# The feed-forward layer of a transformer block by seven products of two-by-two blocks, with its activations kept in DRAM

## The chip, the cores and the metric

The kernel runs on one core of one Trainium2 chip. The metric is the device time of one execution in microseconds (us), the median over several runs.

## What is computed

One encoder layer on x, 512 rows by 2048 columns of float32. First comes attention with forget gates: a normalisation, a projection to q, k, v of 16 heads, per head the scores, a softmax and a weighted sum, and an output projection that is added to x. The result is called x1. The layer then ends with the part that the change is about:

```python
def swiglu(h, w_gu, w_down):
    gu = jnp.einsum('bsd,df->bsf', h, w_gu)          # 512x2048 by 2048x11264
    gate, up = gu[..., :D_FF], gu[..., D_FF:]        # D_FF = 5632
    return jnp.einsum('bsf,fd->bsd', jax.nn.silu(gate) * up, w_down)   # by 5632x2048

h = rmsnorm(x1, ffn_norm_g)
x = x1 + swiglu(h, w_gu, w_down)
```

## The kernel before

All products of matrices are made of three matmuls each. Every float32 operand is split into a rounded part ("hi", type fp32r) and the rest ("lo"), and `three` (L378 to L384) adds hi by hi, hi by lo and lo by hi in PSUM. ACT makes the hi parts of the weights (`split_hi`, L638), DVE the lo parts (`split_lo`, L868: raw minus hi). SP loads the raw weights, 1 MB at a time, into two slots (`load`, L200).

The work is staged in chunks of 4 weight units of 1 MB. After the 16 heads come four chunks of the output projection (d = 0 to 3), each of which ends in `x1_add` (L1030), where DVE adds the product to x in the tile `rows`. In the last of them PE transposes x1 (`transpose_rows`, L418) for the feed-forward. ACT takes sums of squares of x1 (`x1_squares`, L667) for the second normalisation. Its factors are brought to a row by two small matmuls (`rms_b`).

The feed-forward goes through the 5632 hidden columns in NP = 11 parts of 512. For each part there is a gate chunk into the PSUM banks G, an up chunk into the banks X, and a down chunk, which multiplies the part by 512 rows of w_down and adds the result to `rows` (`down_add`, L1085). The gate and up chunks give the hidden values transposed (weights stationary, activations moving), so no transposes are needed between. A gate chunk is scaled on DVE (L1068), put through silu on ACT (L796), scaled on POOL (L369), multiplied by up on DVE (L1076) and split again (L800, L1080). All this runs in a loop, in an order that is written out by hand per engine: each chunk has 16 steps s, and the splits and readers are placed at fixed steps. Each engine waits on semaphores for exactly what it reads. `w_lo_done` lets PE start a unit, and lets SP overwrite the raw slot.

A matmul streams 512 columns past 128 stationary ones. The feed-forward has 11 x 2 x 4 x 4 x 4 x 3 = 4224 of them for gate and up and 11 x 4 x 4 x 4 x 3 = 2112 for down, together 6336.

## Time and profile before

| | |
|---|---|
| median of 3 runs | 2278.01 us (2276.91 to 2278.36) |
| span of the profiled execution, first to last instruction | 2275.4 us |
| around the span, against the median | 2.6 us |
| PE busy | 2266.8 us, 11022 matmuls |
| PE weight loads | 1978.8 us |
| DVE busy | 904.3 us |
| ACT busy | 635.9 us |
| POOL busy | 225.6 us |
| DMA | 222.95 MB, 98 GB/s over the span |

The profile names the profiled execution's span and not its whole time. The median stands 2.6 us above the span, and this is taken as what lies around it. PE means TensorE's matmuls and PEld its weight loads, which overlap them. A busy PE is not PE at its peak, since the ends of matmuls are modelled; what counts is the distance from one start to the next. Lines such as L868 are lines of the kernel, and "out<-in" names the tile written and those read.

### The profile page before, as it was taken

The page shows a single profiled execution, that of the slowest core. Times are in us where ns is not written, and L with a number is a line of the kernel's source. Part 1 is how long each engine was busy: PE and PEld are TensorE (multiplying, and loading weights), DVE is VectorE, ACT ScalarE, POOL GpSimd, SP SyncE. Part 2 cuts the span into 40 slices and gives each one's busy share as a digit, 9 for nine tenths or more (in the row PEclk, how much of TensorE's full clock was granted, in tenths as well). Part 3 has the DMA queues.
Part 4 walks back from the last instruction along what each step waited for, and adds up shares of the span by engine and source line. Part 5 has one row for each costly group of instructions (what it writes and reads, how often), then busy time and mean ns, then how long its engine had stood idle before and what let it go on. Part 6 is the DMA issues. An engine that isn't in the chain of part 4 may idle for free.

```text
span 2275.4 us, 29033 instructions
## 1 busy us (share of the span) xinstructions
PE 2266.8 (100%) x11022; PEld 1978.8 (87%) x11022; DVE 904.3 (40%) x1553; ACT 635.9 (28%) x986; POOL 225.6 (10%) x395
## 2 busy tenths in 40 slices
PE   9999999999999999999999999999999999999999
PEld 8999999999988888888888888888888888888887
DVE  4544444444552242342433333342333334343334
ACT  5433333333442232222222121222222121222211
POOL 1322222222210000000000000000000000000000
PEclk9999999999999999999999999999999999999999
DMA  6333323333252223232232223222222223222223
GB/s 174 85 93 88 92 74 93 87 92 85 81 181 85 101 78 108 81 105 98 87 110 92 92 92 111 92 92 102 84 96 104 97 87 111 92 92 95 95 104 111
DMA packets 190548, 222.95 MB, mean 98 GB/s; under 512 B 8194, under 2 KB 106532, under 8 KB 190516
## 3 DMA queue, kind: packets, MB, share of 16 engines
q1 hardware_dynamic: 190304, 222.49, 30.1%
q8 instruction: 22, 0.36, 0.1%
q14 instruction: 10, 0.08, 0.0%
q10 hardware_dynamic: 212, 0.03, 0.0%
HBM read 218.26 MB, written 4.23 MB: 98 GB/s over the span
## 4 chain that ended last, share of the span: by engine, by line
PE 99%; DMA 0%; DVE 0%; ACT 0%; issue 0%; DVEq 0%
PE gemm L382 17%; PE gemm L384 17%; PE gemm L383 17%; PE aux L383 15%; PE aux L384 15%; PE aux L382 15%; PE aux L446 1%; PE aux L418 1%; PE aux L427 0%; PE aux L428 0%; DMA rows<-in_x 0%; DVE act_lo L873 0%; PE aux L493 0%; PE aux L492 0%; DVE w_lo L868 0%; PE aux L484 0%
## 5 line engine op out<-in xcount | busy, mean ns | idle before, releaser
L868 DVE TENSOR_TENSOR w_lo<-w_raw,w_hi 128x1024 fp32r<-128x1024 f32 (+1 forms) x424 | 483.7, 1154 | 843.0 <-ACT w_hi L638 843.0
L638 ACT ACTIVATE w_hi<-w_raw 128x1024 fp32r<-128x1024 f32 (+1 forms) x424 | 403.3, 988 | 1124.4 <-PE aux L384 650.7
L382 PE MATMUL gemm<-w_hi,act_hi 128*128 128x384 f32 (+2 forms) x1280 | 450.4, 352 | 1.6 <-DVE w_lo L868 1.6
L384 PE MATMUL gemm<-w_hi,act_lo 128*128 128x384 f32 (+2 forms) x1280 | 444.0, 347 | 0.0
L383 PE MATMUL gemm<-w_lo,act_hi 128*128 128x384 f32 (+2 forms) x1280 | 443.9, 347 | 0.0
L382 PE MATMUL aux<-w_hi,work_r 128*128 128x512 f32 x704 | 274.1, 389 | 0.1
L382 PE MATMUL gemm<-act_hi,w_hi 128*128 128x512 f32 x704 | 274.0, 389 | 0.0
L384 PE MATMUL gemm<-act_hi,w_lo 128*128 128x512 f32 x704 | 273.9, 389 | 0.0
L383 PE MATMUL aux<-w_lo,work_r 128*128 128x512 f32 x704 | 273.9, 389 | 0.0
L384 PE MATMUL aux<-w_hi,work_r 128*128 128x512 f32 x704 | 273.9, 389 | 0.0
L382 PE MATMUL aux<-act_hi,w_hi 128*128 128x512 f32 x704 | 273.9, 389 | 0.0
L383 PE MATMUL aux<-act_lo,w_hi 128*128 128x512 f32 x704 | 273.9, 389 | 0.0
L384 PE MATMUL aux<-act_hi,w_lo 128*128 128x512 f32 x704 | 273.9, 389 | 0.0
L383 PE MATMUL gemm<-act_lo,w_hi 128*128 128x512 f32 x704 | 273.9, 389 | 0.0
L382 PEld LDWEIGHTS gemm<-w_hi,act_hi 128*128 128x128 f32 x1280 | 241.0, 188 | 12.5 <-issue 2.0
L383 PEld LDWEIGHTS gemm<-w_lo,act_hi 128*128 128x128 f32 x1280 | 241.1, 188 | 10.4
L384 PEld LDWEIGHTS gemm<-w_hi,act_lo 128*128 128x128 f32 x1280 | 240.7, 188 | 10.0
L1085 DVE TENSOR_TENSOR rows<-aux,rows 128x512 f32<-128x512 f32 x176 | 121.6, 691 | 223.7 <-PE aux L384 223.7
L369 POOL TENSOR_TENSOR work<-work,rms_b 128x512 f32<-128x512 f32 x44 | 57.0, 1294 | 1241.6 <-ACT work L796 1241.6
L382 PEld LDWEIGHTS aux<-w_hi,work_r 128*128 128x128 f32 x704 | 132.1, 188 | 28.2 <-DVE work_r L1080 0.8
L384 PEld LDWEIGHTS aux<-act_hi,w_lo 128*128 128x128 f32 x704 | 132.1, 188 | 27.5
L384 PEld LDWEIGHTS gemm<-act_hi,w_lo 128*128 128x128 f32 x704 | 132.1, 188 | 27.5
(110 smaller groups left out, 1910.3 us busy)
## 6 DMA issues: line engine op xcount, KB each, us to landing
w_raw<-in_ffn_w_gate_up SPq DMA_DIRECT2D x88, 1024.0 KB, 4.8
w_raw<-in_fox_w_in SPq DMA_DIRECT2D x192, 256.0 KB, 3.3
w_raw<-in_ffn_w_down SPq DMA_DIRECT2D x44, 1024.0 KB, 4.9
w_raw<-in_fox_w_out SPq DMA_DIRECT2D x16, 1024.0 KB, 4.9
rows<-in_x SPq DMA_DIRECT2D x8, 1024.0 KB, 7.4
c_key<-c_scratch SPq DMA_DIRECT2D x16, 256.0 KB, 3.2
out_y<-rows SPq DMA_DIRECT2D x3, 1024.0 KB, 4.2
out_y<-rows SPq DMA_DIRECT2D x4, 256.0 KB, 2.3
```

Of the source, the lines that this page charges most:

```text
L369: g.tensor_tensor(silu_t[:, j], silu_t[:, j], rms2_b[:], ALU.mult).then_inc(silu_scaled, 1)
L382: mm(out, a_hi, b_hi, start=first, stop=False)
L383: mm(out, a_hi, b_lo, start=False, stop=False)
L384: return mm(out, a_lo, b_hi, start=False, stop=last)
L418: last = nc.tensor.transpose(X[i][:, bass.ts(t, P)], rows[:, kg, t, bass.ts(i, P)], ident[:])
L446: last = nc.tensor.transpose(dst[:, bass.ts(i - j, P)], prob[:, OFF[i] + P * j:OFF[i] + P * (j + 1)], ident[:])
L638: a.activation(w_hi[:, j % 2, k, 0:width], w_raw[:, j % 2, k, 0:width], ACT.Copy)\
L868: v.tensor_tensor(w_lo[:, j % 2, k, 0:width], w_raw[:, j % 2, k, 0:width], f32(w_hi[:, j % 2, k, 0:width]), ALU.subtract).then_inc(w_lo_do ...
L1085: v.tensor_tensor(rows[:, d, t, :], X[t][:], rows[:, d, t, :], ALU.add).then_inc(bank_free, 1)
```

## The change

The feed-forward is written anew; attention and the output projection stay as they were, but for where their tiles lie.

Both products are cut in two by two blocks: A (activations) in two halves of rows (256) and two halves of the inner dimension, B (weights) in two halves of the inner dimension and two of columns (gate and up for the first product). Instead of eight block products there are seven, in Winograd's form of Strassen's way. With the sums S1 = A21-A22, S2 = S1-A11, S3 = A11-A21, S4 = A12+S2 and T1 = B11+B12, T2 = T1+B22, T3 = B12+B22, T4 = T2+B21, the products are P1 = A11 B11, P2 = A12 B21, P3 = S4 B22, P4 = A22 T4, P5 = S1 T1, P6 = S2 T2, P7 = S3 T3, and the four result blocks are sums of them.

The work is a list `UNITS` of 264 units in 17 rounds, written out without loops. Rounds 0 to 10 make gate and up for 512 hidden columns each; rounds 11 to 16 make down, in three blocks of 8, 7 and 7 steps of the hidden dimension and two halves of columns. A round goes twice over its 8 (or 7) steps of the inner dimension. In the first pass (g = 0) a unit has 3 products and loads 3 blocks of weights of 128x512; in the second (g = 1) it has 4 products and loads all 4 blocks. A product of a unit is 2 x 3 matmuls of 512 columns, so a unit of the first pass has 18 matmuls and one of the second 24, and 132 pairs of them have 5544.

For each unit n: SP loads its blocks into one of four slots once unit n-4 is done; in the second pass DVE makes T1 and T3, later T2 and T4, of them in place (`sums_t1_t3`, `sums_t2_t4`, in DVE's iteration n-2); ACT makes the hi parts (`weights_hi`, `weights_hi_rest`, iteration n-2, three slots); DVE makes the lo parts (`weights_lo`, iteration n-1); PE waits for `f_lo_done`. The iterations of DVE and ACT are tied to these waits alone.

At the end of the first pass of a round ACT and DVE read P1, P2, P3 (6 banks' worth of 512), at the end of the second pass DVE reads P6, P5, P7 and P4 (10 operations of 512). The next round's first pass then applies silu and multiplies (`gate_top`, `gate_bot`, `up_top`, `hidden_top`, `hidden_bot`), PE transposes the result (`hidden_transposes`, 16 per round, 176 in all), and ACT and DVE make its seven forms and their hi and lo parts (`hidden_forms`, `hidden_sums`, `hidden_hi`, `hidden_lo`). The hidden values no longer stay in SBUF: hi and lo forms, 128 x 7 x 256 float32 each, are stored in DRAM from ACT's queue, 4 such stores per round (`store_hi`, `store_lo`), and read back (`load_forms`) per block of down: during the round before the block and the first four units of its own. x1 is stored in DRAM as well and read back into `rows` in rounds 11 and 12, where POOL forms its block sums. The forms of x1 are made in the output projection, with its 64 transposes, and in round 0. The scaling of silu's input by the row factors moves into ACT's scale operand, and POOL's per part work goes. The prefetch of weights over the boundary from the output projection to the feed-forward is left out on ACT and DVE (s >= 12 of d = 3).

All tiles of SBUF lie at written offsets, and areas are shared by tiles that live at different times.

The core of the diff (PE, SP, ACT and DVE of the new feed-forward; the removed loop is that of the kernel above):

```diff
+    NSTEP = FF // (2 * P)
+    BLOCKS = [8, 7, 7]
+    FIRST = [0, 8, 15]
+    R_DOWN = NP
+    NR = NP + 2 * len(BLOCKS)
+    ROUND_K = [8] * NP + [k for k in BLOCKS for _ in range(2)]
+    BASE = [sum(2 * k for k in ROUND_K[:r]) for r in range(NR + 1)]
+    UNITS = [(r, g, j) for r in range(NR) for g in range(2) for j in range(ROUND_K[r])]
...
+            def load_forms(b, g, j):
+                step = FIRST[b] + j
+                sp.wait_ge(hs_hi_stored, 16 * (step + 1))
+                sp.wait_ge(hs_lo_stored, 16 * (step + 1))
+                if g == 0:
+                    sp.dma_start(f32(a_form[:, j, :, 0:3]), dram_forms[step][:, :, 0:3])\
+                        .then_inc(first_ld[j], 16)
+                else:
+                    sp.dma_start(f32(a_form[:, j, :, 3:7]), dram_forms[step][:, :, 3:7])\
...
+            for n in range(NU):
+                r, g, j = UNITS[n]
+                s = n % 4
+                if n in (0, 1):
+                    sp.wait_ge(w_lo_done, 2 * (U_OUT + 15 + n))
+                elif n in (2, 3):
+                    sp.wait_ge(slot_done, 4 * (U_OUT + 13 + n))
+                else:
+                    sp.wait_ge(unit_done, n - 3)
+                if r < R_DOWN:
+                    src, col = w_gu_v[j // 2, j % 2], r * CW
+                else:
+                    step = FIRST[(r - R_DOWN) // 2] + j
+                    src, col = w_down_v[step // 2, step % 2], (r - R_DOWN) % 2 * CW
+                if g == 0:
+                    sp.dma_start(f_raw[:, s, 0:2], src[:, :, 0, col:col + CW]).then_inc(f_ld[s], 16)
+                    sp.dma_start(f_raw[:, s, 2], src[:, 1, 1, col:col + CW]).then_inc(f_ld[s], 16)
+                else:
+                    for half in range(2):
+                        sp.dma_start(f_raw[:, s, 2 * half:2 * half + 2], src[:, half, :, col:col + CW])\
+                            .then_inc(f_ld[s], 16)
+                if n == 3:
+                    store_x1(ND - 1)
...
+                if n == BASE[R_DOWN] + 8:
+                    sp.wait_ge(hidden_tr, 4 * NP)
+                    sp.dma_start(rows[:, 2], dram_x1[2]).then_inc(x1_ld[2], 16)
+                if n == BASE[R_DOWN] + 9:
+                    sp.wait_ge(hs_lo_stored, 16 * (NSTEP - 1))
+                    sp.dma_start(rows[:, 0], dram_x1[0]).then_inc(x1_ld[0], 16)
...
+            def product(n, form, weights, banks, wait_free, last):
+                r, g, j = UNITS[n]
+                hi, lo = f_hi[:, n % 3, weights], f_lo[:, n % 4, weights]
+                for t in range(2):
+                    if j == 0:
+                        wait_free(r, t)
+                    st_hi = a_form[:, j, 0, form, bass.ts(t, P)]
+                    st_lo = a_form[:, j, 1, form, bass.ts(t, P)]
+                    mm(banks[t][:], st_hi, hi, start=j == 0, stop=False)
+                    mm(banks[t][:], st_hi, lo, start=False, stop=False)
+                    i = mm(banks[t][:], st_lo, hi, start=False, stop=j == ROUND_K[r] - 1)
+                    if last and t == 1:
+                        i.then_inc(unit_done, 1)
+                    elif j == ROUND_K[r] - 1:
+                        i.then_inc(product_done, 1)
...
+            for n in range(NU):
+                r, g, j = UNITS[n]
+                b = (r - R_DOWN) // 2
+                pe.wait_ge(f_lo_done, n + 1)
...
+                if g == 0:
+                    product(n, A11, 0, bank_a, free_p1, False)
+                    product(n, A12, 1, bank_b, free_p2, False)
+                    product(n, S4, 2, bank_c, free_p3, True)
...
+                    if 1 <= r <= R_DOWN and j in (2, 3):
+                        hidden_transposes(r, j - 2)
+                else:
+                    if j == 0:
+                        product(n, S1, 0, bank_d, free_p5, False)
+                        product(n, S2, 3, bank_a, free_p6, False)
+                    else:
+                        product(n, S2, 3, bank_a, free_p6, False)
+                        product(n, S1, 0, bank_d, free_p5, False)
+                    product(n, S3, 1, bank_b, free_p7, False)
+                    product(n, A22, 2, bank_c, free_p4, True)
...
+            def hidden_hi(r, i):
+                step = 2 * (r - 1) + i
+                act.wait_ge(form_done, 8 + step + 1)
+                if step == 0:
+                    act.wait_ge(x1_stored[3], 16)
+                else:
+                    act.wait_ge(hs_hi_stored, 16 * step)
+                    act.wait_ge(hs_lo_done, step)
+                a.activation(hs_hi[:], (fa_a, fa_b)[i][:, 0:7], ACT.Copy).then_inc(hs_hi_done, 1)
...
+            def store_hi(r, i):
+                step = 2 * (r - 1) + i
+                act.wait_ge(hs_hi_done, step + 1)
+                act.dma_start(dram_forms[step][:, 0], f32(hs_hi[:])).then_inc(hs_hi_stored, 16)
...
+            x1_squares(ND - 1, 3)
+            weights_hi(0)
+            weights_hi(1)
+            for n in range(NU):
+                r, g, j = UNITS[n]
+                hidden = 1 <= r <= R_DOWN
+                last = j == ROUND_K[r] - 1
+                if g == 0:
+                    if j == 0 and hidden:
+                        gate_bot(r - 1)
+                    if j == 5 and hidden:
+                        store_hi(r, 0)
+                else:
+                    if j == 1 and hidden:
+                        store_hi(r, 1)
+                if n + 2 < NU:
+                    weights_hi(n + 2)
+                if g == 0 and last:
+                    read_p1(r)
+                    if r < R_DOWN:
+                        read_p3(r)
+                if n + 2 < NU and UNITS[n + 2][1] == 1:
+                    weights_hi_rest(n + 2)
+                if g == 0:
...
+                    if j == 3 and hidden:
+                        hidden_forms(r, 0)
+                    if j == 4 and hidden:
+                        hidden_hi(r, 0)
+                        hidden_forms(r, 1)
+                    if j == 5 and hidden:
+                        store_lo(r, 0)
+                    if j == 6 and hidden:
+                        hidden_hi(r, 1)
+                else:
+                    if j == 2 and r < R_DOWN:
+                        gate_top(r)
+                    if j == 5 and hidden:
+                        store_lo(r, 1)
...
+            def weights_lo(n):
+                g = UNITS[n][1]
+                dve.wait_ge(f_hi_done, HI_COUNT[n])
+                v.tensor_tensor(f_lo[:, n % 4, 0:3 + g], f_raw[:, n % 4, 0:3 + g],
+                                f32(f_hi[:, n % 3, 0:3 + g]), ALU.subtract).then_inc(f_lo_done, 1)
+            def sums_t1_t3(n):
+                dve.wait_ge(f_ld[n % 4], LANDED[n])
+                f = f_raw[:, n % 4]
+                v.tensor_tensor(f[:, 0:2], f[:, 0:2], f[:, 1:4:2], ALU.add).then_inc(t_step, 1)
+            def sums_t2_t4(n):
+                f = f_raw[:, n % 4]
+                dve.wait_ge(t_step, 3 * T_COUNT[n] + 1)
+                v.tensor_tensor(f[:, 3], f[:, 0], f[:, 3], ALU.add).then_inc(t_step, 1)
+                dve.wait_ge(t_step, 3 * T_COUNT[n] + 2)
+                v.tensor_tensor(f[:, 2], f[:, 3], f[:, 2], ALU.add).then_inc(t_step, 1)
+            def read_p2(r):
+                for t in range(2):
+                    dve.wait_ge(p1_read, 2 * r + t + 1)
+                    wait_product(dve, r, False, 2 + t)
+                    v.tensor_tensor(c_one[:, t], bank_b[t][:], u_two[:, t], ALU.add).then_inc(p2_read, 1)
...
+                for t in range(2):
+                    wait_product(dve, r, True, t)
+                    v.tensor_tensor(u_two[:, t], bank_a[t][:], u_two[:, t], ALU.add).then_inc(p6_read, 1)
+                for t in range(2):
+                    dve.wait_ge(p6_read, 2 * r + t + 1)
+                    wait_product(dve, r, True, 2 + t)
+                    v.tensor_tensor(h_bot[:, t], bank_d[t][:], u_two[:, t], ALU.subtract).then_inc(p5_read, 1)
+                for t in range(2):
+                    dve.wait_ge(p5_read, 2 * r + t + 1)
+                    wait_product(dve, r, True, 4 + t)
+                    v.tensor_tensor(c_neg[:, t], bank_b[t][:], h_bot[:, t], ALU.subtract).then_inc(c22_done, 1)
+                    v.tensor_tensor(u_two[:, t], bank_b[t][:], u_two[:, t], ALU.add).then_inc(p7_read, 1)
+                for t in range(2):
+                    dve.wait_ge(p7_read, 2 * r + t + 1)
+                    wait_product(dve, r, True, 6 + t)
+                    v.tensor_tensor(u_two[:, t], bank_c[t][:], u_two[:, t], ALU.add).then_inc(p4_read, 1)
...
+            x1_add(ND - 1, 3)
+            weights_lo(0)
+            for n in range(NU):
+                r, g, j = UNITS[n]
+                hidden = 1 <= r <= R_DOWN
+                last = j == ROUND_K[r] - 1
+                sums = n + 2 < NU and UNITS[n + 2][1] == 1
+                if sums:
+                    sums_t1_t3(n + 2)
+                if n + 1 < NU:
+                    weights_lo(n + 1)
+                if sums:
+                    sums_t2_t4(n + 2)
+                if g == 0:
+                    if r == 0:
+                        if j == 1:
...
+                        if j == 2:
...
+                        if j == 3:
...
+                    if hidden:
+                        if j == 0:
+                            up_top(r - 1)
+                        if j == 1:
+                            hidden_top(r - 1)
+                        if j == 2:
+                            hidden_bot(r - 1)
+                        if j == 3:
+                            hidden_sums(r, 0)
+                        if j == 4:
+                            hidden_lo(r, 0, slice(0, 7), True)
+                        if j == 5:
+                            hidden_sums(r, 1)
+                    if r > R_DOWN:
+                        if j == 0:
+                            finish_x4(r - 1)
+                        if r == NR - 1 and j == 1:
+                            last_sums(r - 1)
+                        if r == NR - 1 and j == 2:
+                            last_bottom(r - 1)
+                    if last:
+                        if r < R_DOWN:
+                            read_p2(r)
+                        else:
+                            add_p2_p3(r)
+                else:
+                    if r >= R_DOWN and j == 1:
+                        add_p1(r)
+                    if hidden and j == 3:
+                        hidden_lo(r, 1, slice(0, 3), False)
+                    if hidden and j == 4:
+                        hidden_lo(r, 1, slice(3, 7), True)
+                    if last and r < R_DOWN:
+                        second_pass_read(r)
+                    if last and r >= R_DOWN:
+                        down_read(r)
+                        if r < NR - 1:
+                            add_p4(r)
```

## Rows read from the trace of the kernel before

**Rows 1.** The page: busy time by engine; the chain that ended last, by engine.
```profile
PE 2266.8 (100%) x11022; PEld 1978.8 (87%) x11022; DVE 904.3 (40%) x1553; ACT 635.9 (28%) x986; POOL 225.6 (10%) x395
...
PE 99%; DMA 0%; DVE 0%; ACT 0%; issue 0%; DVEq 0%
```

**Rows 2.** The waits of PE: who waited for whom, total, times, longest.
```profile
PE gemm L538 <- DVE causal_r L1003: 3.1, 1, 3.1
PE gemm L382 <- DVE w_lo L868: 1.6, 1, 1.6
```

**Rows 3.** Busy time by stretch: output projection, feed-forward.
```profile
core 0: us, PE busy (x) PEld busy (x) DVE busy (x) ACT busy (x) POOL busy (x), PEclk, DMA share, GB/s
...
690.00:840.00 150.00, 150.00 (x697) 125.12 (x695) 49.58 (x54) 45.38 (x72) 0.00 (x0) 1.00 0.27 92
...
860.00:2230.00 1370.00, 1369.88 (x6044) 1133.93 (x6042) 497.91 (x543) 306.57 (x340) 56.95 (x44) 1.00 0.28 96
```

**Rows 4.** Timeline of PE: start, duration; 30 matmuls apart, then 48 matmuls apart.
```profile
757.01 0.39 PE L383 MATMUL gemm<-w_lo,act_hi 128*128 128x512 f32 x1
...
763.81 0.39 PE L383 MATMUL gemm<-w_lo,act_hi 128*128 128x512 f32 x1
...
1500.13 0.39 PE L382 MATMUL aux<-w_hi,work_r 128*128 128x512 f32 x1
...
1511.01 0.39 PE L382 MATMUL aux<-w_hi,work_r 128*128 128x512 f32 x1
```

**Rows 5.** The chain in order of time: 16 transposes of x1 and the last steps.
```profile
838.45 1.75 PE aux L418 x16
...
2271.97 0.69 DVE rows L1085
```

**Rows 6.** Groups by line and shape: busy, mean ns of one, idle before.
```profile
L868 DVE TENSOR_TENSOR w_lo<-w_raw,w_hi 128x1024 fp32r<-128x1024 f32 x296 | 361.7, 1240 | 706.9 <-ACT w_hi L638 706.9
...
L868 DVE TENSOR_TENSOR w_lo<-w_raw,w_hi 128x768 fp32r<-128x768 f32 x128 | 122.0, 955 | 136.1 <-ACT w_hi L638 136.1
...
L369 POOL TENSOR_TENSOR work<-work,rms_b 128x512 f32<-128x512 f32 x44 | 57.0, 1294 | 1241.6 <-ACT work L796 1241.6
```

**Rows 7.** Timeline of DVE and ACT: back to back, and the end of the output projection.
```profile
2225.97 0.68 DVE L1076 TENSOR_TENSOR qk_raw<-aux,work 128x512 f32<-128x512 f32 x1
2226.57 0.68 DVE L1080 TENSOR_TENSOR work_r<-qk_raw,work_r 128x512 fp32r<-128x512 f32 x1
...
2240.49 2.36 DVE L868 TENSOR_TENSOR w_lo<-w_raw,w_hi 128x1024 fp32r<-128x1024 f32 x2 [0.46 <-ACT w_hi L638]
...
839.64 2.73 DVE L873 SCALAR_TENSOR_TENSOR act_lo<-aux,gain,act_hi 128x512 fp32r<-128x512 f32 x4 [2.95 <-ACT act_hi L651]
...
833.04 0.69 DVE L1030 TENSOR_TENSOR rows<-gemm,rows 128x512 f32<-128x512 f32 x1 [2.03 <-PE gemm L384]
...
833.76 0.63 ACT L667 ACTIVATE junk_act<-rows 128x512 f32<-128x512 f32 x1 [2.00 <-DVE rows L1030]
...
834.39 1.04 ACT L638 ACTIVATE w_hi<-w_raw 128x1024 fp32r<-128x1024 f32 x1
```

**Rows 8.** DMA: a load issued at 1506.40, by stretch (columns of rows 3), landings.
```profile
1505.02 1.22 DVE L868 TENSOR_TENSOR w_lo<-w_raw,w_hi 128x1024 fp32r<-128x1024 f32 x1
...
1506.40 0.37 SPq L200 DMA_DIRECT2D w_raw<-in_ffn_w_gate_up  x1
...
1509.40:1510.40 1.00, 1.00 (x6) 0.82 (x5) 0.55 (x1) 0.55 (x1) 0.00 (x0) 1.00 1.02 397
...
2242.00:2243.00 1.00, 1.00 (x7) 0.81 (x6) 1.00 (x2) 0.00 (x0) 0.00 (x0) 1.00 1.02 379
...
w_raw<-in_ffn_w_gate_up SPq DMA_DIRECT2D x88, 1024.0 KB, 4.8
...
out_y<-rows SPq DMA_DIRECT2D x3, 1024.0 KB, 4.2
...
DMA to landing us min/median/max: 2.8/3.7/9.0
```

739 lines of the change are left out of this document (446 added, 293 removed).

## The prediction

> **What bounds the kernel now.** I read the shares of the page and the chain first: PE is busy for the whole span and holds 99% of the chain that ended last [rows 1]. The waits of PE confirm it: after the first microseconds of the kernel it waits for nobody [rows 2]. By stretch, PE is full in the output projection and in the feed-forward, at a granted clock of 1.00, while DVE is busy 36% and ACT 22% of the feed-forward, and DMA runs at 96 GB/s [rows 3]. The timeline then gives the price of a matmul. The starts of 30 matmuls in the output projection span 6.80 us and those of 48 in the feed-forward 10.88 us [rows 4], so one costs 0.2267 us, whichever operand is stationary. 6336 of them are 1436 us, all on the path. Only fewer matmuls, or cheaper ones, can help, unless another engine takes over.
>
> **What the change removes.** 6336 - 5544 = 792 matmuls: 792 x 0.2267 = 179.5 us. The new matmuls have the shape and roles of the output projection's (activations stationary, 512 columns of weights moving), hence the same price. The two matmuls of `rms_b` go: 0.5 us. POOL's scaling and DVE's L1068 and L1076 lay beside PE and give nothing. The 4 MB of x1 that go to DRAM in the output projection lie beside PE too, at the 92 GB/s that DMA has there [rows 3].
>
> **What it adds on PE.** 176 transposes of hidden values, at 1.75 us for 16 [rows 5]: 19.2 us. The 64 transposes of x1 stay. PE's work thus falls by 179.5 + 0.5 - 19.2 = 160.8 us. A unit of the first pass is now 18 x 0.2267 = 4.08 us, one of the second 5.44 us, a round with 8 of each and 16 transposes 77.9 us.
>
> **DVE's cover.** The gaps between back-to-back starts are what counts: 0.60 us for 512 columns [rows 7], 1.14 for 1024 (a pair is 2.36, one 1.22), 0.66 for the three-operand form. At this slope 1536 columns take 1.67 us and 2048 take 2.2. Where a following instruction waits, I take the full 0.69 and 1.24, and 1.8 and 2.3 by the two shapes of rows 6. A unit of the first pass costs DVE 1.67 us against PE's 4.08. One of the second costs 1.14 + 2.2 + 0.74 + 0.6 = 4.7 against 5.44. Per round these are 51 us. The reads of products (12 x 0.6), up_top (1.2), the hidden product (4 x 0.66), the sums of forms (8 short ones, 3.0) and their lo parts (3.9) add 18. So DVE needs 69 of PE's 78 us, where it had 36%. ACT needs some 40 (1.5 or 2.1 us per unit, at 1.04 per 1024 columns [rows 7], and some 11 for reads, silu and forms). On average neither binds; in places DVE does.
>
> **Where a round loses time.** I walk one. In the second pass's steady part, the load of unit n+2 is issued when unit n-1 starts (0.2 us for PE's end, as a matmul runs 0.39 [rows 4], and 0.16 from the release to SP's issue [rows 8]) and lands 4.8 us later [rows 8], 5.15 in all. That is 0.3 us before unit n starts. Then come T1/T3 (1.14) and the lo part of n+1 (2.3), ready 3.2 us into a unit of 5.44: no stall, 2.2 us of slack. At the change from first to second pass the units are only 4.08 long, so the load of unit 8 (counted from the round's start) lands 1.07 us into unit 6. T1/T3 goes ahead of unit 7's lo part in DVE's queue, which ends at 4.0: just in time. In unit 7 DVE still has T2/T4 of unit 8 until 1.2 us, then T1/T3 of unit 9 and the lo part of unit 8 (2.2, behind ACT's `weights_hi_rest` at 2.35), ready at 4.7: PE waits 0.6. Then T2/T4 of 9 and `read_p2` delay the lo part of 9 by another 0.5 us. That is 1.1 us per round, 17 rounds: 18.7 us. In the down rounds the reader there has 4 operations instead of 2, 1.2 us more: in rounds 12 to 16, 6.0 us. At the end of a second pass the ten reads fit before their banks are wanted, and I count nothing.
>
> **The stores.** Per round ACT issues four stores of 0.917 MB. A busy load moves up to 397 GB/s and a store 379, with the 16 engines' share at 1.02 [rows 8], so either fills them. One store takes 2.4 us of them. `store_hi` is issued about 0.5 us into unit 5, just as the load of unit 8 is, and they share the engines. The load lands some 2.4 us later, at 3.5 us into unit 6, in front of DVE's queue; the lo part of unit 7 waits behind it, and PE with it. This is the one place in the round without slack: 2.4 us x 11 rounds (1 to 11) = 26.4 us. The other stores meet loads too, in places with 1 to 2 us of slack, or while PE stands already: nothing. Bounds: 0 if the store is served after the load, and 5 us per round if both stores go ahead of it. The Trainium skill, DMA: Bandwidth & Descriptors, section "Issuing engines are not separate DMA queues", says that transfers issued from SP and ACT run on the same 16 engines and interleave. By it the stores cannot slip past the loads; if they could, the 26.4 would fall away.
>
> **The forms' way back.** In round 10 loads of forms join: 0.79 MB beside 0.79 MB of weights in a unit of 4.08 us is 387 GB/s, all that rows 8 show, and the stores come on top. I take 5 us more. In round 11 four units want 1.84 MB in 4.08 us. Then SP waits for a store before it reloads x1, with weights queued behind; the reload lands some 8 us into the first pass's last unit, and POOL needs two sums of 1024 columns (at 1.29 per 512 [rows 6], 5.2 us), for which `add_p2_p3` waits on DVE. I take 7 us more. Rounds 12 and 14 load the next blocks' forms at 360 to 390 GB/s: 1.5 each, 3. Bounds for this part: 3 to 40 us, as its demand is at the engines' limit. The same page, section "Specifications", puts HBM's limit per core at some 358 GB/s; the trace shows 397, which decides. By 358 the four units of 387 GB/s would each take 0.3 us more, 1 us in all.
>
> **Both ends.** At the start, the first unit's weights are not split ahead any more. After the last matmul of the output projection come x1's last add and its squares (0.72 and 0.63 from start to next start), hi of 1536 (1.5) and lo (1.8) [rows 6, 7], with handshakes 5.1 us in which PE stands (3 to 7). At the end, the last read is behind ten others: PE's last unit starts at 0, the P7 reads end at 6.1 us, then eight more operations bring the last output to 11.1, where PE was done at 5.6. The gap is 5.5 us against 0.7 now [rows 5]: 4.8 more. The last store is 256 KB as before.
>
> **The sum.** 2275.4 - 160.8 + 5.1 + 18.7 + 6.0 + 26.4 + 5 + 7 + 3 + 4.8 = 2190.6 us of span. The median stands 2.6 us above the profiled span now, so 2193 us.
>
> **The rivals.**
>
> (a) The stores and form loads stay hidden. Then 26.4 + 15 fall away: 2152 us. For it: DMA's mean would be only some 260 GB/s (242 MB of weights, 81 of forms and 8 of x1 in 1260 us). Against it: order in DVE's queue leaves no room at unit 6.
>
> (b) DVE becomes the bound in patches. With full durations and handshakes in place of the gaps a second-pass unit costs it 5.1 us, and a round 75 of 78; every lump then shows. At 3 us more per round, 17 rounds: 51 us, 2244 us. For it: DVE waits on its own results several times per unit. Against it: the back-to-back rows.
>
> (c) Slower: the loads' landing sets the pace. Two units can't be shorter than landing + 0.36 + 1.14 + 2.3, because load n+2 waits for unit n-2 and lo n+1 stands behind it. At 4.8 us this gives 4.3 per unit. It binds from a landing of 7.1 us, and at 9.0, the longest seen with a full queue [rows 8], a second-pass unit takes 6.4 instead of 5.44: 132 x 0.96 = 127 us, 2320 us. It passes the present time from a landing of about 8.4. For it: such landings occur when several transfers queue. Against it: outside rounds 10 to 14 the engines would be some 60% full.
>
> (d) PE's waits cost its clock. For it: the new feed-forward has waits where the old had none. Against it: a wait of 1.6 us near the start [rows 2] left the granted clock at 1.00, and the waits above are mostly shorter. Only the 5 us at the start is long; at 1.2 GHz for as long again it costs under 3 us, inside the range.
>
> **How the numbers follow.** Chances: forecast 0.50, (a) 0.18, (b) 0.24, (c) 0.06, others 0.02. The range reaches to (a) with half of the 18.7 gone too, 2143, and a little past (b), 2248, which leaves out (c) and the edges of (a) and (b). All but (c) are faster by far more than 0.2% (4.6 us, what this kernel's runs can tell from no change): faster 0.93, same 0.01, slower 0.06.
>
> **What would show it.** Matmuls 11022 - 6336 - 2 + 5544 + 176 = 10404, at 0.2267 us within a unit. The waits of PE would be led by `f_lo`, and lie at the start of units 7, 8 and 9 of each round, 3 to 4 us together, with 5 us at the first unit. Landings would be 4.8 us in quiet parts and 7 or more beside the first store. Rounds 1 to 9 would take 80 to 83 us each. The prediction fails if the gap between matmuls within a unit grows, if DVE's operations run longer than their shapes here, or if landings stay above 7 us throughout.

## The result, and the profile after

The changed kernel takes **2245.3 us** (median; 2234.7 to 2246.8) against 2277.5 in the runs beside it: ratio 0.9849, interval 0.9828 to 0.9870, so 1.5% faster. The profiled execution has a span of 2244.7 us, where the sum gave 2190.6. The gain is 32 us, not 85. One of the four runs took 2234.7 us and the others 2244.2 to 2246.8, so by the two intervals a difference between this kernel and one of the runs below is good to some 6 us (an estimate). Where a difference is smaller than that, I go by the traces.

The page of the changed kernel: busy time by engine; GB/s in 40 slices; the chain by engine.

```profile
PE 2155.1 (96%) x10404; PEld 1864.5 (83%) x10404; DVE 1520.2 (68%) x2092; ACT 911.7 (41%) x1203; POOL 181.8 (8%) x356
...
GB/s 176 86 94 75 93 89 80 88 89 93 75 182 108 99 128 175 212 202 236 224 207 229 232 190 234 233 193 230 235 188 359 316 220 322 300 178 315 277 177 182
...
PE 70%; DVE 15%; DMA 12%; issue 1%; SPq 1%; ACT 0%; DVEq 0%; ACTq 0%
```

The matmuls are the 10404 of the forecast, but PE has fallen from 99% of the chain [rows 1] to 70%. Slices 31 to 35, with 220 to 359 GB/s, are rounds 10 to 12, where loads of forms join.

The waits of PE, the two waits of DVE for the weights' landing, and the landings (KB each, median us):

```profile
PE aux L714 <- DVE f_lo L1350: 69.0, 46, 5.4
PE gemm L714 <- DVE rows L1431: 3.1, 1, 3.1
...
PE gemm L513 <- DVE w_lo L1129: 3.0, 1, 3.0
PE gemm L714 <- DVE u_two L1387: 1.5, 2, 1.3
```

```profile
DVE f_raw L1356 <- DMA f_raw<-in_ffn_w_gate_up: 84.8, 28, 6.1
...
DVE f_raw L1356 <- DMA f_raw<-in_ffn_w_down: 45.2, 15, 9.1
```

```profile
f_raw<-in_ffn_w_gate_up SPq DMA_DIRECT2D x264, 512.0 KB, 4.6
f_raw<-in_ffn_w_down SPq DMA_DIRECT2D x132, 512.0 KB, 5.3
...
forms_scratch<-hs_hi ACTq DMA_DIRECT2D x22, 896.0 KB, 5.1
```

Where [rows 2] had no wait of PE in the feed-forward, it now waits for `f_lo` 46 times, and behind `f_lo` stands T1/T3 (L1356), which waits for the load.

By stretch: output projection; feed-forward; then four stretches of 3.4 or 6.8 us (columns of [rows 3]).

```profile
690.00:840.00 150.00, 145.58 (x667) 120.68 (x665) 61.66 (x71) 54.38 (x76) 0.00 (x0) 0.99 0.35 113
860.00:2230.00 1370.00, 1299.71 (x5626) 1054.46 (x5625) 1109.26 (x1077) 574.70 (x558) 14.94 (x7) 0.98 0.71 238
```

```profile
837.90:844.70 6.80, 4.41 (x10) 3.47 (x11) 5.09 (x3) 3.29 (x3) 0.00 (x0) 0.50 0.62 244
957.40:960.80 3.40, 3.40 (x10) 2.61 (x9) 3.40 (x3) 2.78 (x3) 0.00 (x0) 0.50 0.12 44
1206.60:1210.00 3.40, 3.40 (x10) 2.63 (x9) 3.40 (x3) 3.38 (x3) 0.00 (x0) 0.50 0.17 66
1814.20:1821.00 6.80, 5.85 (x14) 4.43 (x15) 6.76 (x9) 2.11 (x2) 0.00 (x0) 0.50 0.03 8
```

In these four the granted clock is 0.50, which is 1.2 GHz, and matmuls start 0.43 us apart. [Rows 3] had 1.00 throughout. There are 15 such stretches from the feed-forward's start to its last matmul, together 28.5 us longer than at 2.4 GHz.

How one round loses its time, on the timeline of round 4, at the start of units 6 and 7 (the last two of the first pass). SP's line gathers eight issues, of which the first is the load of unit 8:

```profile
1192.21 0.33 ACTq L1061 DMA_DIRECT2D forms_scratch<-hs_hi  x1
...
1194.09 18.44 SPq L370 DMA_DIRECT2D f_raw<-in_ffn_w_gate_up  x8
...
1194.28 0.35 ACTq L1066 DMA_DIRECT2D forms_scratch<-fa_a_lo  x1
...
1202.36 1.23 DVE L1356 TENSOR_TENSOR f_raw<-f_raw 128x1024 f32<-128x1024 f32 x1 [4.99 <-DMA f_raw<-in_ffn_w_gate_up]
1203.50 1.75 DVE L1350 TENSOR_TENSOR f_lo<-f_raw,f_hi 128x1536 fp32r<-128x1536 f32 x1
...
1205.31 0.50 PE L714 MATMUL aux<-f_hi,a_form 128*128 128x512 f32 x1 [3.09 <-DVE f_lo L1350]
...
1207.41 0.63 PE L715 MATMUL gemm<-f_lo,a_form 128*128 128x512 f32 x1
```

The load is issued at 1194.09 between two stores and lands at 1202.3, 8.2 us later. It comes in two halves, and 8.2 us is the time to the second one's landing. In rounds 1 to 9 this takes 7.6 to 9.1 us, a mean of 8.2; with nearly empty stores (told below) it takes 5.2 to 6.2, a mean of 5.6. The 4.6 of the list above is for a half. DVE stands for 4.99 us, though the lo part of unit 7, which needs nothing of that load, could run. PE waits 3.1 us, and 1.3 us after it resumes its clock halves until 1210.0.

To split the 54.1 us between forecast and measured span, I take the distances between starts of consecutive matmuls. What exceeds 0.2267 is a wait; in stretches at a clock of 0.50, 0.2 us per matmul are the clock's.

| term | forecast | measured | over |
| --- | --- | --- | --- |
| output projection's last matmul starts (before: 832.61) | 832.61 | 835.19 | +2.6 |
| a round of 8 and 8 units without its waits | 77.9 | 77.97 | +0.1 |
| wait at the first unit | 5.1 | 4.9 | -0.2 |
| waits in the 17 rounds | 66.1 | 88.8 | +22.7 |
| halved clock | 0 | 28.5 | +28.5 |
| tail, beyond what it was | 4.8 | 5.0 | +0.2 |

The 88.8 us by place, from the same distances:

| wait before | forecast | after | with small stores and form loads |
| --- | --- | --- | --- |
| the first pass's last unit | 26.4 | 47.6 | 14.8 |
| the second pass's units 0 and 1 | 24.7 | 16.0 | 33.2 |
| the second pass's unit 3 | 0 | 10.5 | 3.5 |
| others (rounds 10 to 14, transposes) | 15 | 15 | 5.7 |

The last column is of a run told below. Places are rounded, so that they add up to 0.3 us more than the 88.8.

### The profile page after: what moved, and what is told of

It reads as the page before. It is cut to its first block, busy times and chain, and to the rows that moved or that the text cites. A ratio compares the mean times of both kernels' runs of the same rounds, so it can differ in the third digit from the quotient of the medians.

```text
span 2244.7 us, 27898 instructions
## 1 busy us (share of the span) xinstructions
PE 2155.1 (96%) x10404; PEld 1864.5 (83%) x10404; DVE 1520.2 (68%) x2092; ACT 911.7 (41%) x1203; POOL 181.8 (8%) x356
## 4 chain that ended last, share of the span: by engine, by line
PE 70%; DVE 15%; DMA 12%; issue 1%; SPq 1%; ACT 0%; DVEq 0%; ACTq 0%
PE gemm L513 11%; PE gemm L515 11%; PE gemm L514 11%; DVE f_lo L1350 6%; PE gemm L714 6%; PE gemm L715 6%; PE gemm L716 6%; DMA f_raw<-in_ffn_w_gate_up 6%; PE aux L714 5%; PE aux L716 4%; PE aux L715 4%; DMA f_raw<-in_ffn_w_down 4%; DVE f_raw L1356 3%; DMA forms_scratch<-fa_b_lo 2%; DVE f_raw L1361 1%
## 5 line engine op out<-in xcount | busy, mean ns | idle before, releaser
L1350 DVE TENSOR_TENSOR f_lo<-f_raw,f_hi 128x2048 fp32r<-128x2048 f32 (+1 forms) x264 | 532.7, 2024 | 52.8 <-ACT f_hi L998 33.5
L513 PE MATMUL gemm<-w_hi,act_t 128*128 128x384 f32 (+2 forms) x1280 | 451.6, 353 | 3.0 <-DVE w_lo L1129 3.0
L514 PE MATMUL gemm<-w_lo,act_t 128*128 128x384 f32 (+2 forms) x1280 | 444.7, 347 | 0.0
L515 PE MATMUL gemm<-w_hi,act_t 128*128 128x384 f32 (+2 forms) x1280 | 444.6, 347 | 0.0
L714 PE MATMUL gemm<-f_hi,a_form 128*128 128x512 f32 x1056 | 418.8, 397 | 4.6 <-DVE rows L1431 3.1
L715 PE MATMUL gemm<-f_lo,a_form 128*128 128x512 f32 x1056 | 417.0, 395 | 0.0
L716 PE MATMUL gemm<-f_hi,a_form 128*128 128x512 f32 x1056 | 416.1, 394 | 0.0
L714 PE MATMUL aux<-f_hi,a_form 128*128 128x512 f32 x792 | 322.7, 407 | 70.3 <-DVE f_lo L1350 69.0
L716 PE MATMUL aux<-f_hi,a_form 128*128 128x512 f32 x792 | 313.8, 396 | 0.0
L715 PE MATMUL aux<-f_lo,a_form 128*128 128x512 f32 x792 | 313.6, 396 | 0.0
L714 PEld LDWEIGHTS aux<-f_hi,a_form 128*128 128x128 f32 x792 | 150.8, 190 | 125.3 <-DVE f_lo L1350 95.4
L513 PEld LDWEIGHTS gemm<-w_hi,act_t 128*128 128x128 f32 x1280 | 241.4, 189 | 13.8 <-issue 3.4
L1005 ACT ACTIVATE f_hi<-f_raw 128x1024 fp32r<-128x1024 f32 x132 | 140.2, 1062 | 275.7 <-DVE f_raw L1363 275.7
L515 PEld LDWEIGHTS gemm<-w_hi,act_t 128*128 128x128 f32 x1280 | 241.4, 189 | 10.1
L1356 DVE TENSOR_TENSOR f_raw<-f_raw 128x1024 f32<-128x1024 f32 x132 | 161.1, 1220 | 130.3 <-DMA f_raw<-in_ffn_w_gate_up 84.8
L714 PEld LDWEIGHTS gemm<-f_hi,a_form 128*128 128x128 f32 x1056 | 202.7, 192 | 48.9 <-DVE rows L1431 3.6
L716 PEld LDWEIGHTS gemm<-f_hi,a_form 128*128 128x128 f32 x1056 | 202.1, 191 | 43.2
L1001 ACT ACTIVATE f_hi<-f_raw 128x1024 fp32r<-128x1024 f32 x132 | 139.8, 1059 | 222.4 <-DVE f_raw L1356 218.9
```

What stands on the lines that cost most here:

```text
L513: mm(out, a_hi, b_hi, start=first, stop=False)
L514: mm(out, a_hi, b_lo, start=False, stop=False)
L515: return mm(out, a_lo, b_hi, start=False, stop=last)
L714: mm(banks[t][:], st_hi, hi, start=j == 0, stop=False)
L715: mm(banks[t][:], st_hi, lo, start=False, stop=False)
L716: i = mm(banks[t][:], st_lo, hi, start=False, stop=j == ROUND_K[r] - 1)
```

## The experiments

Two theories for the missing 52 us: the **stores**' contention costs more than I took; or the **waits' clock**: each wait halves the clock afterwards, and that is the larger part. A third concerns the **order in DVE's queue**. Each edit is made to the changed kernel; ratios are against the kernel before (2276.9 to 2278.2 us in these runs).

**Work for PE in the waits (e1_fill).** 20 extra matmuls before the first unit, and 11 (2.5 us) before the first pass's last unit in rounds 1 to 12 and 14. They write a bank that is free then.

```diff
+                if n == 0:
+                    pe.wait_ge(xform_read, 12)
+                    fill(20, j)
+                if g == 0 and j == ROUND_K[r] - 1 and (1 <= r <= R_DOWN + 1 or r == R_DOWN + 3):
...
+                    fill(11, j)
                 pe.wait_ge(f_lo_done, n + 1)
```

> Edit: while PE would wait, it runs matmuls whose result nobody reads: 20 ahead of the first unit of the feed-forward, 11 (2.5 us) ahead of the last unit of the first pass in rounds 1 to 12 and 14. No wait of another engine changes. In the changed kernel PE waits 4.7 us at the first and 2.6 to 5.3 us at the others, and after 11 of these 14 waits the granted clock is halved for 3.4 or 6.8 us and matmuls start 0.427 us apart instead of 0.227; all such time together lost 30 us. Theory 1 (the wait itself lowers the clock): the matmuls fill idle time, the waits stay in length (PE's start of the following unit does not move), and the clock's loss goes: 20 to 28 us faster than the changed kernel's 2245, so 2217 to 2225. Theory 2 (the clock falls for another reason, such as the load of the DMA and DVE at that place): the clock falls as before and the time is 2240 to 2248.

Measured: 2232.7 us (0.9795, 0.9779 to 0.9811). Timeline of PE at the first unit:

```profile
832.65 4.70 PE L724 MATMUL aux<-a_form 128*128 128x512 f32 x20
837.53 0.50 PE L714 MATMUL aux<-f_hi,a_form 128*128 128x512 f32 x1 [0.18 <-DVE f_lo L1363]
```

By stretch, over most of rounds 1 to 9, this kernel and then the changed one:

```profile
970.00:1636.00 666.00, 654.79 (x2911) 532.59 (x2910) 551.34 (x552) 303.71 (x304) 0.00 (x0) 1.00 0.67 222
```

```profile
970.00:1636.00 666.00, 637.48 (x2801) 520.19 (x2800) 548.94 (x549) 302.50 (x303) 0.00 (x0) 0.98 0.67 220
```

The clock is 1.00 where PE had matmuls in its waits: the halved clock's 28.5 us fall to 4.4. But the waits, fillers counted as waits, grow from 88.8 to 105.4. The slowed matmuls had covered the waits before the second pass's units 0 and 1, which come out at 0.6 and 0.4 us, near the forecast's 0.6 and 0.5, once the clock stays up. So the clock's net price is 12.6 us by the medians, and 7.5 by the two profiled executions (24.1 of halved clock less, 16.6 of waits more); either is short of what was expected.

**Stores and form loads nearly without bytes (e2_small_stores).** Only one of the seven forms is stored, and one of each three or four loaded. All instructions and waits stay.

```diff
-                act.dma_start(dram_forms[step][:, 0], f32(hs_hi[:])).then_inc(hs_hi_stored, 16)
+                act.dma_start(dram_forms[step][:, 0, 0:1], f32(hs_hi[:, 0:1])).then_inc(hs_hi_stored, 16)
```

> Edit: each store of hidden forms, and each load of them, moves one form of seven (of three, of four), so the output is not the reference's; all waits stay. Theory 1 (the first pair of stores shares the 16 DMA engines with the load of the first second-pass unit, whose sums stand ahead of the lo part of the last first-pass unit in DVE's queue): the 2.7 to 3.9 us that PE waits before the last first-pass unit in rounds 1 to 9 fall to 0 to 0.8 (0.8 is what round 0 shows, which has no stores), the clock then stays at 1.00 there, and with the small form loads rounds 10 to 14 lose little too: 30 + 25 + 20 = some 65 to 80 us faster than the changed kernel, 2165 to 2180. Theory 2 (DVE's own work in those units is the cause, stores or not): the waits stay above 2 us, and the gain is under 20 us, from the form loads alone.

Measured: 2185.8 us (0.9595, 0.9579 to 0.9611), 59.5 below the changed kernel. The waits of PE and the stretch:

```profile
PE aux L714 <- DVE f_lo L1350: 39.2, 46, 4.7
```

```profile
970.00:1636.00 666.00, 657.38 (x2934) 537.55 (x2933) 578.00 (x572) 315.83 (x316) 0.00 (x0) 1.00 0.60 191
```

Rounds 1 to 9 take 79.5 to 80.9 us. The wait before the first pass's last unit falls from a mean of 3.2 us there to 0.6, so the contention takes 2.6 of it, just what the load of unit 8 lands earlier (8.2 us to 5.6); I had 2.4. The clock stays up without any filler. What remains is the last column of the table above: 57.2 us of waits, where the forecast has 24.7 without stores.

**The lo part of the next unit ahead of T1/T3 (e3_lo_first)**, in the first pass's last two units:

```diff
+                lo_first = g == 0 and j >= ROUND_K[r] - 2
-                if sums:
+                if sums and not lo_first:
                     sums_t1_t3(n + 2)
                 if n + 1 < NU:
                     weights_lo(n + 1)
+                if sums and lo_first:
+                    sums_t1_t3(n + 2)
```

> Edit: in DVE's iterations of the last two units of a first pass the lo part of the next unit's weights comes before T1 and T3 of the unit after it. Theory 1 (order in DVE's queue passes the load's late landing on to PE): the wait before the last first-pass unit goes to 0 in all rounds; T1 to T4 of the first second-pass unit end as late as before, so its lo part is late in its stead, by 1 to 2.5 us; per round 1.5 us are gained and the clock's loss mostly goes: 25 to 40 us faster, 2205 to 2220. Theory 2 (the late landing costs its full length wherever DVE takes it): the wait only moves one unit on, and the time is 2238 to 2248.

Measured: 2233.2 us (0.9800, 0.9784 to 0.9816). Timeline of PE, round 3, unit 8 and its second product:

```profile
1122.39 0.50 PE L714 MATMUL aux<-f_hi,a_form 128*128 128x512 f32 x1 [2.31 <-DVE f_lo L1350]
...
1125.16 0.50 PE L714 MATMUL aux<-f_hi,a_form 128*128 128x512 f32 x1 [1.11 <-ACT u_two L1018]
```

The wait before the first pass's last unit is gone, but 1.7 to 3.2 us come before the next unit, up to 1.3 within it (its second product writes the bank that ACT reads P1 from) and 0.5 before the one after. The load of unit 8 is late, whoever is first in the queue; the order decided which unit paid. It gives 12.1 us, less than was expected.

**Every store doubled (e4_double_stores)**, each form stored a second time to a region that nothing reads.

```diff
                 act.dma_start(dram_forms[step][:, 0], f32(hs_hi[:])).then_inc(hs_hi_stored, 16)
+                act.dma_start(dram_extra[step][:, 0], f32(hs_hi[:])).then_inc(hs_hi_stored, 16)
```

> Edit: each of the 44 stores of hidden forms is issued twice, the second time to a tensor that nobody reads, and its readers wait for both. Theory 1 (stores delay the loads by their time on the DMA engines, 2.4 us each): the first pair becomes four of 0.917 MB, 4.7 us more per round in front of or beside the loads, most of which PE sees: 3.5 to 6 us per round, 11 rounds, 40 to 65 us slower than the changed kernel, 2285 to 2310. Theory 2 (stores are not what delays): under 10 us slower.

Measured: 2337.5 us (1.0261, 1.0244 to 1.0278), 92 above the changed kernel. Its waits of PE, and round 4 where the load of unit 8 is issued and lands:

```profile
PE aux L715 <- DVE f_lo L1354: 142.8, 56, 8.6
```

```profile
1220.94 23.65 SPq L371 DMA_DIRECT2D f_raw<-in_ffn_w_gate_up  x8
...
1233.94 1.23 DVE L1360 TENSOR_TENSOR f_raw<-f_raw 128x1024 f32<-128x1024 f32 x1 [9.72 <-DMA f_raw<-in_ffn_w_gate_up]
```

The landing goes from 8.2 to 13.0 us, 4.8 for two more stores, which is 2.4 each (12.5 in the mean of rounds 1 to 9, 2.2 each). The wait before unit 7 becomes 7.0 to 8.4 us in these rounds, and 2 to 4 us appear before the second pass's unit 3, behind the second pair of stores. The 92 us over 44 added stores are 2.1 each, halved clock included: hardly any of an added store is hidden.

**The first unit's weights split ahead of x1's last work (e5_start).**

```diff
-            x1_squares(ND - 1, 3)
             weights_hi(0)
             weights_hi(1)
+            x1_squares(ND - 1, 3)
...
-            x1_add(ND - 1, 3)
             weights_lo(0)
+            x1_add(ND - 1, 3)
```

> Edit: at the start of the feed-forward ACT makes the hi parts of the first two units before the squares of x1's last block, and DVE the lo part of the first before x1's last add. Theory 1 (the 4.9 us that PE waits there come from this order, and the halved clock after it, 2.0 us, from the wait): both go, 6 to 7 us faster than the changed kernel's 2245. Theory 2 (the loads of the first units or the forms of x1 would hold PE anyway): under 2 us.

Measured: 2238.6 us (0.9828, 0.9812 to 0.9845). 6.7 us by the medians, as expected but hardly more than their spread. The trace shows what came of it: PE's wait before the first unit falls from 4.9 to 2.3 us and is not gone, and the clock stays at 1.00 behind it. From the output projection's last matmul to the start of round 1 it takes 5.1 us less.

**These edits together, with 8 fillers before unit 8 (e6_combined)**; the lo part is also first in the second pass's unit 0.

> Edit: the start of e5; in DVE's last two iterations of a first pass and the first of a second the lo part comes before T1 and T3; PE runs 8 matmuls that nobody reads ahead of the first unit of the second pass in rounds 1 to 14. If the causes add (order of the queue, clock, start): 6.5 from the start, 15 from the order, 18 from the clock: 2200 to 2210. If order and clock are one gain counted twice (the lo-first kernel still lost 22 us to the clock, the one with filling matmuls 4): 2212 to 2222.

Measured: 2228.5 us (0.9790, 0.9773 to 0.9806), clock 0.997. The gains of 12.6, 12.1 and 6.7 us don't add: 16.8 together. I read clock and order as two sides of one late load; the spread of the three gains is wide, and this was not tested apart. Waits are 100.2 us now, halved clock 3.3.

**Only the form loads small (e7_small_form_loads)**, all stores whole.

```diff
-                    sp.dma_start(f32(a_form[:, j, :, 0:3]), dram_forms[step][:, :, 0:3])\
+                    sp.dma_start(f32(a_form[:, j, :, 0:1]), dram_forms[step][:, :, 0:1])\
```

> Edit: the loads of hidden forms for down move one form of three or four; the stores stay whole. The output is not the reference's. Theory 1 (the form loads take what DMA has left in rounds 10 to 12 and 14, as those rounds wait 4.5, 11, 7.6 and 4 us longer than their like): 15 to 22 us faster than the changed kernel, and nothing changes in rounds 1 to 9. Theory 2 (rounds 11 and 12 wait for the reload of x1 and POOL's sums, not for forms): 3 to 9 us.

Measured: 2231.5 us (0.9796, 0.9780 to 0.9813). 13.8 us: rounds 10, 12 and 14 go from 88.4, 88.0 and 74.8 us to 84.5, 82.6 and 71.8. Round 11 goes only from 95.4 to 93.1: its rest is the reload of x1 and the base sums, and even with small stores PE waits 3.3 us there within the second pass's unit 0 (the row for `rows` L1431) and 2.3 before unit 1.

**The first lo store one step of ACT later, on e6_combined (e8_combined_lo_later).**

```diff
-                    if j == 5 and hidden:
-                        store_lo(r, 0)
                     if j == 6 and hidden:
+                        store_lo(r, 0)
                         hidden_hi(r, 1)
```

> Edit: as e6, and the first lo store of a round is issued one ACT iteration later, after the first second-pass unit's load has landed. If the pair of stores delays that load by what both of them move: its landing comes 2 us earlier, and the wait before the first second-pass unit falls by 1 to 2 us in rounds 1 to 11: 10 to 20 us faster than e6. If the later store delays the next load as much, or the read of P1 that waits for it: within 4 us of e6.

Measured: **2220.7 us** (0.9753, 0.9737 to 0.9770), 7.7 below e6_combined. Round 4: the first store, the load of unit 8, its landing, the second store.

```profile
1181.75 0.33 ACTq L1071 DMA_DIRECT2D forms_scratch<-hs_hi  x1
...
1183.28 13.49 SPq L370 DMA_DIRECT2D f_raw<-in_ffn_w_gate_up  x8
...
1188.94 1.23 DVE L1365 TENSOR_TENSOR f_raw<-f_raw 128x1024 f32<-128x1024 f32 x1 [0.36 <-DMA f_raw<-in_ffn_w_gate_up]
...
1191.66 0.34 ACTq L1076 DMA_DIRECT2D forms_scratch<-fa_a_lo  x1
```

With the second store behind the load of unit 8, the load lands in 5.5 to 6.5 us, a mean of 5.9, and rounds 1 to 9 take 80.3 to 83.3 us. So of the 2.6 us by which the pair delays this load, the first store, 1.5 to 1.9 us ahead of it, has 0.3, and the second, issued 0.2 us behind it, has 2.3.

**The same without fillers (e9_no_fill).**

> Edit: e8 without the 8 matmuls that fill the wait. In e8 PE waits no longer than these 8 matmuls (1.8 us) before the second pass in most rounds, so they may now be the wait. If they are, and the wait under them is shorter than what lowers the clock: 0.5 to 1 us less per round, 2208 to 2216. If the clock falls again in most rounds: 2222 to 2235.

Measured: 2222.7 us (0.9773, 0.9752 to 0.9794). Halved clock 14.2 us against 8.1, waits 83.0 against 89.1: the fillers no longer matter beyond the spread. The second product of unit 8 waits for ACT's read of P1. Timeline of PE there, rounds 1 and 5:

```profile
953.35 0.50 PE L714 MATMUL aux<-f_hi,a_form 128*128 128x512 f32 x1 [1.81 <-ACT u_two L1018]
...
1282.33 0.50 PE L714 MATMUL aux<-f_hi,a_form 128*128 128x512 f32 x1 [2.21 <-ACT u_two L1018]
```

Between starts these waits are 2.0 and 2.1 us in rounds 1 and 2, and behind both the clock fell to 0.50; in rounds 3 to 9 they are 1.9 to 2.4 us, and it stayed at 1.00.

**Forms stored once, as float32, and split after the reload (e10_raw_forms)**, on e5_start with the lo part first: half the bytes, but ACT and DVE split each form twice, once per use.

```diff
-                a.activation(hs_hi[:], (fa_a, fa_b)[i][:, 0:7], ACT.Copy).then_inc(hs_hi_done, 1)
-                act.dma_start(dram_forms[step][:, 0], f32(hs_hi[:])).then_inc(hs_hi_stored, 16)
+                act.dma_start(dram_forms[step], (fa_a, fa_b)[i][:, 0:7])\
+                    .then_inc((hs_hi_stored, hs_lo_stored)[i], 16)
...
+                    a.activation(a_form[:, j, 0, k], f32(a_form[:, j, 1, k]), ACT.Copy).then_inc(raw_hi, 1)
...
+                    v.tensor_tensor(a_form[:, j, 1, k], f32(a_form[:, j, 1, k]), f32(a_form[:, j, 0, k]),
+                                    ALU.subtract).then_inc(raw_lo, 1)
```

> Edit: the start of e5 and the order of e6, and the hidden forms go to DRAM once, as float32, instead of as hi and lo parts: 2 stores of 0.917 MB per round instead of 4, form loads of half the size; hi and lo parts are made after the reload, in rounds 11, 13 and 15, by ACT and DVE. The output is the reference's. Theory 1 (stores beside the first second-pass loads are the largest cost, form loads the next): per round 2 to 3 us less wait than in the changed kernel in rounds 1 to 10, the clock stays at 1.00 there, rounds 10 and 12 to 14 lose 15 us less; the split adds 3.3 us of DVE work per step in rounds 11, 13 and 15, some 5 to 10 us where DVE is full. 2245 - 7 - 30 - 20 - 12 + 8 = 2175 to 2195. Theory 2 (halving the bytes does not help, since the time of the landing is set by latency): 2215 to 2230.

Measured: 2226.6 us (0.9776, 0.9763 to 0.9790). Rounds 1 to 10 take 80.2 to 81.6 us at a clock of 1.00: little of the contention is left. The stores were halved and moved at once here, so their shares aren't told apart. But rounds 11, 13 and 15, before whose end forms are split, take 102.3, 82.0 and 82.1.

**The splits spread over earlier units (e11_raw_spread).** They are either late in those rounds, or simply too much for DVE.

```diff
-                return [(0, j + 1)] * (j + 1 < k) + [(1, j)] * (j < 6)
-            return [(1, 6 + j - 2)] * (2 <= j < 2 + k - 6)
+                return [(b, 0, j + 2), (b, 1, j - 1)] * (1 <= j <= k - 3)
+            return [(b, 1, k - 3 + j - 2)] * (2 <= j <= 4)
```

> Edit: e10, with the splitting of reloaded forms spread otherwise: the first three first-pass forms of a block are split in the second pass of the round before, the others two units ahead, the second-pass forms one per unit from unit 1 on and the last three in the second pass. In e10 rounds 1 to 10 took 80.2 to 81.6 us, but rounds 11, 13 and 15 took 102, 82 and 82 us against 95, 71 and 71 of the changed kernel, with waits for the lo parts of forms in front of units 1 and 6. If these come from the place of the splits alone: rounds 13 and 15 fall to 71 to 74 and round 11 to 88 to 94, 2195 to 2207. If DVE's added work is what costs (0.86 and 1.14 us in each of 8 units, some 16 us per block): at most 8 us are gained, 2218 or more.

Measured: 2231.1 us (0.9796, 0.9783 to 0.9809). Rounds 13 and 15 get shorter (78.1, 79.2), but 10, 12 and 14 longer (88.1, 87.2, 76.7). Most second-pass units that hold a split have a wait of 1.9 to 2.5 us behind them, the others less: DVE's work is the price.

**ACT reads P1 before it splits weights (e12_raw_read_first)**, on e11_raw_spread.

```diff
+                if g == 0 and last:
+                    read_p1(r)
                 if n + 2 < NU:
                     weights_hi(n + 2)
-                if g == 0 and last:
-                    read_p1(r)
-                    if r < R_DOWN:
-                        read_p3(r)
+                if g == 0 and last and r < R_DOWN:
+                    read_p3(r)
```

> Edit: e11, and at the end of a first pass ACT reads P1 before it makes the first hi parts of the unit after next, not behind them. In e10 PE waits 9.8 us over 11 places for this read. If it is the last of PE's waits there: up to 1 us per round less, 8 to 15 us faster than e11. If the lo part of the next unit is as late anyway: within 4 us of e11.

Measured: **2219.7 us** (0.9745, 0.9732 to 0.9758), 11.4 below e11_raw_spread. By stretch, rounds 3 to 9 and then round 13:

```profile
1077.00:1636.00 559.00, 554.38 (x2475) 453.14 (x2474) 463.73 (x467) 244.45 (x252) 0.00 (x0) 1.00 0.63 208
...
1908.00:1986.00 78.00, 69.14 (x295) 54.56 (x294) 68.48 (x65) 35.72 (x34) 0.00 (x0) 1.00 0.54 169
```

In rounds 3 to 9 PE is busy 554 of 559 us, 79.3 to 80.2 us a round. In round 13 DVE is busy 68.5 of 78 us and PE waits for `f_lo` in seven places, though DMA carries 169 GB/s. This version and e8_combined_lo_later (2220.7) can't be told apart; both beat both kernels.

## Why the prediction was wrong in size, step by step

**What held.** The saving on PE: 10404 matmuls, and 77.97 us per round without its waits. The start (4.9 us) and the tail (5.0). DVE's load, 69 us of a round: it is busy 548.94 of 666 us over most of rounds 1 to 9. The sign, and the place of most waits: led by `f_lo`, before units 7, 8 and 9. SP's load of unit 8 lands in 6.0 us in round 4 with small stores from ACT, in 8.2 beside two whole ones, in 13.0 beside four; this agrees with the rule of the Trainium skill that I weighed (DMA: Bandwidth & Descriptors, "Issuing engines are not separate DMA queues"). The measured 2245.3 us lies inside the stated range, 2143 to 2248, but at its upper end, which stood there for (b) and not for what happened.

**The step that failed: "PE's waits cost its clock", set at nothing, "under 3 us, inside the range".** The ledger has 28.5 us of halved clock, the largest single term missed. I argued from one wait of 1.6 us without effect [rows 2] and let it stand for the waits of 3 us that my own sum put in eleven rounds. The fillers of e1_fill show that the waits bring it, and that it is worth 7.5 to 12.6 us net, because slow matmuls cover waits behind them. The Trainium skill, TensorE: Matmul & The Clock Gate, section "HAM oscillation — how this bites in real kernels", describes a like case, a wait for DMA ahead of a short group of matmuls that brings the clock down group after group. The trace agrees in ten of the twelve rounds 1 to 12, at 1.4 to 6.0 us each, though some 80 us of matmuls stand between the waits here, and it does not in rounds 2 and 3 (waits of 2.8 and 2.7 us).

**The clock alone is not the 52 us.** e2_small_stores splits them otherwise: 34 stay when stores and form loads carry almost no bytes (2185.8 against (a)'s 2152), nearly all of it waits (57.2 us where I had 24.7), and 18 are what the bytes cost beyond the 41.4 of the sum (59.5), halved clock included. So beside the clock the margin that follows failed too.

**"Just in time" was not.** I had the lo part of unit 7 end at 4.0 of unit 6's 4.08 us and counted nothing. With small stores it is 0.2 to 1.2 us late in rounds 1 to 9 and up to 1.6 later: 14.8 us in all. This timeline of round 16, which has no stores, shows it:

```profile
2187.72 1.23 DVE L1356 TENSOR_TENSOR f_raw<-f_raw 128x1024 f32<-128x1024 f32 x1 [5.84 <-DMA f_raw<-in_ffn_w_down]
2188.87 1.75 DVE L1350 TENSOR_TENSOR f_lo<-f_raw,f_hi 128x1536 fp32r<-128x1536 f32 x1
...
2208.42 1.22 DVE L1444 TENSOR_TENSOR rows<-rows,junk_act 128x1024 f32<-128x1024 f32 x1
2209.55 1.22 DVE L1445 TENSOR_TENSOR rows<-junk_act,rows 128x1024 f32<-128x1024 f32 x1
```

I took 4.8 us from issue to landing, the median of a load of 1 MB in one piece. The new unit's two halves take 5.9 us here (5.6 in the mean of rounds 1 to 9 with small stores), and land 2.0 us into unit 5 (the last but one) instead of 1.07.

**The store term was right in size, 2.4 forecast, 2.6 measured per round**, and it came on top of that lateness. In part this is luck. I had `store_hi` issued with the load and charged its 2.4 us. It is issued 1.9 us ahead of the load and costs 0.3; the 2.3 are `store_lo`'s, 0.2 us behind the load (e8_combined_lo_later), which I had among the stores that cost nothing. The second pair, also set at nothing, costs 7.0 us at the second pass's unit 3 (10.5 against 3.5 with small stores).

**Transition and down reader: 24.7 forecast.** In round 16 the waits before the second pass's first two units are 0.7 and 1.6 us, the 2.3 forecast. Left out were `add_p1`'s two operations, the last two lines above: with T1/T3 and a lo part behind them, PE waits 0.7 us in most of the down rounds.

**The forms' way back: 15 forecast.** Its demand on the engines cost 13.8 us (e7_small_form_loads), clock and all. Round 11's reload and base sums stay as waits of 3.3 and 2.3 us with small stores, near the 7 that I took for that round. The trace shows more there: while POOL's sums run, two of DVE's operations that take 0.7 us elsewhere take 2.9 and 2.7.

```profile
1808.05 3.14 POOL L501 TENSOR_TENSOR rows<-rows 128x1024 f32<-128x1024 f32 x1 [941.26 <-DMA rows<-x_scratch]
...
1808.85 2.89 DVE L1361 TENSOR_TENSOR f_raw<-f_raw 128x512 f32<-128x512 f32 x1
...
1811.77 2.72 DVE L1363 TENSOR_TENSOR f_raw<-f_raw 128x512 f32<-128x512 f32 x1
```

`add_p2_p3` behind them waits for POOL anyway, so what this cost PE was not separated.

**The rivals.** (a) is out: taking the stores and form loads away gave 59.5 us against the 41.4 of the sum, and still left 2185.8, not 2152. (b) had the right time, 2244 us, for the wrong reason: in rounds 2 and 3 the second pass's steady part has waits of 0.2 us at most, so a second-pass unit does fit DVE at 5.44 us. (c) did not happen. e4_double_stores is slower than the kernel before, by 2.6%, but its waits lie mostly at units 7 and 11 of a round and not in every unit of the second pass, as (c) has them. (d) did happen, and had no chance of its own.

**Open.** Why the clock falls after one wait of 2.0 us (e9_no_fill, round 1) and not after another of 3.8 (e5_start, round 12) was not found. The 2.6 us ahead of the feed-forward come from the first 20 us of the kernel: PE waits 3.0 us for `w_lo` in the place of 1.6 [rows 2], and the clock is halved for 3.4 us behind it.

```profile
14.65 0.42 PE L513 MATMUL gemm<-w_hi,act_t 128*128 128x400 f32 x1 [3.01 <-DVE w_lo L1129]
...
15.30:18.70 3.40, 3.40 (x12) 3.38 (x11) 1.54 (x3) 0.44 (x3) 0.00 (x0) 0.51 1.06 383
```

This differs from execution to execution of the same code: in e5_start and e12_raw_read_first that wait is 3.7 and 4.3 us and the output projection's last matmul starts at 835.3 and 836.3, in the runs with a wait of 1.6 to 2.1 us at 831.8 to 832.9. Why the wait differs was not looked into. A third pair of weight slots, which would take the late load off the path, wasn't tried, as SBUF is full.

## What to carry to other kernels

When a change shortens PE's stretches, write the helper engine's queue beside the shortest of them, and look for the instruction that waits for a transfer while ready work stands behind it: there a transfer of another queue that is issued with it costs nearly its full time on the DMA engines, and a margin of 0.1 us is none. Take a landing time from loads cut the same way. Price a wait of PE above some 2 us with a halved clock behind it, but check what the slow matmuls then cover before expecting it back.
